# Sinks as a score column, split order of the first gate slot after an attention, and one product for a task's row numbers

## The reference

```python
def sink_softmax_values(s, sink, v):
    sk = jnp.broadcast_to(sink.astype(F32).reshape(1, KVC, REPC, 1, 1), s.shape[:-1] + (1,))
    p = jax.nn.softmax(jnp.concatenate([s, sk], axis=-1), axis=-1)[..., :-1]
    return jnp.einsum('bgrqk,bkgd->bqgrd', p.astype(v.dtype), v)

def merge_branches(h, oA, oB, oC, w_gate_l, w_branch_l, w_out_l):
    o = jnp.stack([oA, oB, oC], axis=2)
    p = jnp.einsum('btnc,ncd->btnd', o, w_branch_l)
    g = jax.nn.sigmoid((h @ w_gate_l).reshape(B, T, N_BRANCH, D_MODEL))
    return jnp.sum(g * p, axis=2) @ w_out_l

for e in range(N_EXP):
    y = y + gates[..., e:e + 1] * swiglu(h, w_ex_gate[i, e], w_ex_up[i, e], w_ex_down[i, e])
```

## Time and profile before

| | us |
|---|---|
| median of 3 runs | 1545.44 (1542.32 to 1548.37) |
| the profiled execution, its own time | 1546.68 |
| its span in the trace | 1544.3 |
| TensorE busy | 1490.6 (97%) |
| DVE busy | 944.2 (61%) |
| ACT busy | 787.4 (51%) |
| mean rate of transfers | 222 GB/s |

### The profile page before, as it was taken

How to read it: one execution, slowest core, us unless ns; L and a number is a source line. 1 busy time by engine, 2 the same in 40 slices (tenths; PEclk the granted TensorE clock), 3 DMA queues, 4 the chain that set the end, 5 groups by cost and what they waited for, 6 DMA issues and landing times.

```text
span 1544.3 us, 22244 instructions
## 1 busy us (share of the span) xinstructions
PE 1490.6 (97%) x8684; PEld 1312.1 (85%) x8684; DVE 944.2 (61%) x1133; ACT 787.4 (51%) x904; POOL 55.7 (4%) x54
## 2 busy tenths in 40 slices
PE   5999999999999999999999999998999999999997
PEld 4788969679999999997889696898888888888875
DVE  3642275655654254346522756556888898988988
ACT  4433263453532242234343544535778777787875
POOL 0100000000000000000000000000000000000002
PEclk8999999999999999999999999999999999999999
DMA  9754374573763444244333654534899999999994
GB/s 332 249 174 149 104 249 161 193 244 113 239 180 110 142 120 136 96 139 166 120 116 110 204 178 145 184 113 165 311 379 382 372 374 374 371 388 370 372 373 171
DMA packets 236028, 342.36 MB, mean 222 GB/s; under 512 B 8629, under 2 KB 156766, under 8 KB 235694
## 3 DMA queue, kind: packets, MB, share of 16 engines
q1 hardware_dynamic: 227392, 313.32, 59.3%
q0 software_dynamic: 6496, 24.69, 4.4%
q10 hardware_dynamic: 2062, 3.24, 0.6%
HBM read 325.74 MB, written 15.47 MB: 221 GB/s over the span
## 4 chain that ended last, share of the span: by engine, by line
PE 86%; DVE 6%; DMA 3%; ACT 3%; issue 1%; ACTq 0%; SPq 0%; DVEq 0%
PE ps L632 26%; PE ps L634 25%; PE ps L633 25%; PE ps L649 2%; DVE wlo L2004 2%; DMA raw<-in_w_ada_dram 2%; PE ps L809 1%; ACT whi L1439 1%; DMA raw<-in_w_gate_dram 1%; PE ps L681 1%; PE ps L1026 1%; DVE wlo L1625 1%; PE ps L715 1%; PE ps L826 1%; ACT whi L1208 0%
## 5 line engine op out<-in xcount | busy, mean ns | idle before, releaser
L632 PE MATMUL ps<-hhi,whi 128*128 128x384 f32 x864 | 291.1, 337 | 3.5 <-DVE wlo L1625 2.2
L634 PE MATMUL ps<-hhi,wlo 128*128 128x384 f32 x864 | 288.8, 334 | 0.0
L633 PE MATMUL ps<-hlo,whi 128*128 128x384 f32 x864 | 288.7, 334 | 0.0
L1625 DVE TENSOR_TENSOR wlo<-raw,whi 128x2048 fp32r<-128x2048 f32 x66 | 151.0, 2289 | 173.8 <-ACT whi L1208 173.5
L2004 DVE TENSOR_TENSOR wlo<-raw,whi 128x2048 fp32r<-128x2048 f32 (+1 forms) x81 | 179.7, 2228 | 28.6 <-ACT whi L1439 27.3
L1439 ACT ACTIVATE whi<-raw 128x2048 fp32r<-128x2048 f32 (+1 forms) x81 | 150.5, 1867 | 52.6 <-PE ps L634 52.3
L2004 DVE TENSOR_TENSOR wlo<-mraw,whi 128x2048 fp32r<-128x2048 f32 (+2 forms) x81 | 160.7, 1993 | 23.5 <-ACT whi L1439 23.1
L632 PEld LDWEIGHTS ps<-hhi,whi 128*128 128x128 f32 x864 | 162.2, 188 | 9.1 <-issue 3.2
L632 PE MATMUL ps<-whi,xgh 128*128 128x512 f32 (+1 forms) x432 | 163.8, 379 | 4.8 <-DVE wlo L2004 3.7
L633 PEld LDWEIGHTS ps<-hlo,whi 128*128 128x128 f32 x864 | 162.2, 188 | 0.3
L1439 ACT ACTIVATE whi<-mraw 128x2048 fp32r<-128x2048 f32 (+2 forms) x81 | 136.1, 1681 | 51.5 <-PE ps L634 51.1
(11 more groups left out here) (326 smaller groups left out, 2451.9 us busy)
## 6 DMA issues: line engine op xcount, KB each, us to landing
raw<-in_w_ada_dram SPq DMA_DIRECT2D x82, 512.0 KB, 5.7
raw<-in_w_ex_up_dram SPq DMA_DIRECT2D x27, 1024.0 KB, 7.4
raw<-in_w_ex_down_dram SPq DMA_DIRECT2D x27, 1024.0 KB, 6.6
raw<-in_w_gate_dram SPq DMA_DIRECT2D x48, 512.0 KB, 4.6
raw<-in_w_in_dram SPq DMA_DIRECT2D x44, 512.0 KB, 5.5
raw<-in_w_ex_gate_dram SPq DMA_DIRECT2D x18, 1024.0 KB, 7.3
mraw<-in_w_ex_gate_dram SPq DMA_DIRECT2D x18, 1024.0 KB, 7.9
mraw<-in_w_ex_down_dram SPq DMA_DIRECT2D x18, 1024.0 KB, 8.3
```

The lines of the kernel that those rows point to most:

```text
L632: pe.matmul(out, s[0], m[0], start=first, stop=False, **kw)
L633: pe.matmul(out, s[0], m[1], start=False, stop=False, **kw)
L634: return pe.matmul(out, s[1], m[0], start=False, stop=last, **kw)
L1625: dve.tensor_tensor(wlo[:, n % RING, :], raw[:, n % RING, :], whi[:, n % RING, :].bitcast(F32), ALU.subtract).then_inc(lo_done, 1)
```

## The change

Five edits.

1. *Sinks.* A new ACT step `sinks(l)`, after the last gate of branch 1, writes the eight sinks into spare columns of PSUM banks 0 to 3 with four instructions; TensorE waits for `sinks_set` before the first windowed scores. The scores of a step are placed so that the column of their sink is next to them (`score_col`, `with_sink`), the maximum and the exponentials run over 129 or 385 columns, and the sum contains the sink. L1788, L1789, L1349 and L1797 go. `ebuf` has 388 columns, and the weights start at column 1 or 257.
2. *Last exponentials.* `exps(11)` comes right after `pt_copy(9)`, before the output copy of the third head (before: after it).
3. *First gate slot.* ACT makes `whi` in two halves (`gate_hi`, one per block of 128 outputs), the first after `pt_copy(10)` (in layer 0's windowed attention after `pt_copy(11)`), the second after the last `pt_copy`; `whi` of the second gate slot comes behind `ada_end`. TensorE waits for the first half only (`gate_high`) and runs the first block as 16 products on `whi`, then, after `lo_done`, 8 on `wlo`.
4. *After a norm.* The first channel's products on `hhi` come first, behind `first_high`, and those on `hlo` after `first_ready`, in layer 1's input projection and in the dense SwiGLU.
5. *Row numbers.* The comparisons also multiply by the token number, DVE adds the three matrices, and TensorE makes one product with a column of ones.

```diff
+        def score_col(t):
+            return (1, 1, 122, 123)[t // 3] + (T - P if t % 3 == 0 and t else 0)
+        def weight_col(t):
+            return 1 + (T - P if t % 3 == 0 and t else 0)
+        def with_sink(c, t):
+            nk = P if t % 3 == 0 else T
+            return slice(c - 1, c + nk) if t < 3 else slice(c, c + nk + 1)
...
                 if l:
+                    pe.wait_ge(lo_done, split_count(win_slot(l, 0) + 1))
+                    pe.wait_ge(first_high, 2)
+                    w = [x[:, 0, :] for x in slot(win_slot(l, 0), 4)]
+                    for b in range(BLK):
+                        for half in range(2):
+                            pe.matmul(proj_out(Q_A)[:, b, :], hhi[:, 0, b * P:(b + 1) * P], w[half], start=(half == 0), stop=False)
                     pe.wait_ge(first_ready, 2)
-                    pe.wait_ge(lo_done, split_count(win_slot(l, 0) + 1))
                     for b in range(BLK):
-                        products(Q_A, b, (0,))
+                        pe.matmul(proj_out(Q_A)[:, b, :], hlo[:, 0, b * P:(b + 1) * P], w[0], start=False, stop=False)
...
+            def high_first(l, o, w, x):
+                out = ps[:, 2 * gate_pair(l, gate_slot(l, o, 0, 0)), 0:T]
+                pe.wait_ge(gate_high, 2 * l + o)
+                for k in range(KD):
+                    if o == 1 and k == 6:
+                        ada_end(2 + 2 * l)
+                    pe.matmul(out, w[0][:, k, 0:P], x[0][:, k, :], start=(k == 0), stop=False)
+                    pe.matmul(out, w[0][:, k, 0:P], x[1][:, k, :], start=False, stop=False)
+                pe.wait_ge(lo_done, split_count(gate_slot(l, o, 0, 0) + 1))
+                for k in range(KD):
+                    if o == 1 and k == 2:
+                        head_squares(l)
+                    pe.matmul(out, w[1][:, k, 0:P], x[0][:, k, :], start=False, stop=(k == KD - 1))
...
-                for b in range(BLK):
-                    mm = pe.matmul(ps[:, 7, 0:1], gat[:, b, :], slotc[:, 2 * P + b:2 * P + b + 1], start=(b == 0),
-                                   stop=(b == BLK - 1))
-                mm.then_inc(idx_mm, 1)
+                pe.matmul(ps[:, 7, 0:1], gat[:, 0, :], ones[:, 0:1], start=True, stop=True).then_inc(idx_mm, 1)
...
+            def gate_hi(l, o, j):
+                n = gate_slot(l, o, 0, 0)
+                if j == 0:
+                    raw_wait(act, n)
+                    if last_user(n, of_ada) >= 0:
+                        act.wait_ge(mm_done, last_user(n, of_ada) + 1)
+                dst, src = [x[:, n % RING, :].rearrange("p (k c) -> p k c", k=KD)[:, :, j * P:(j + 1) * P] for x in (whi, raw)]
+                act.activation(dst, src, copy).then_inc(hi_done if j else gate_high, 1)
...
+            def sinks(l):
+                act.wait_ge(gate_evac, 12 * l + 8)
+                for p in range(2):
+                    for hp, c in ((0, slice(0, T + 2, T + 1)), (2, slice(T + 122, T + 124))):
+                        x = act.activation(ps[:, 2 * p:2 * p + 2, c],
+                                           sinkr[:, l, 2 * hp:2 * hp + 4].rearrange("p (h m) -> p m h", m=2), copy)
+                x.then_inc(sinks_set, 1)
...
-                    if kind == 1:
-                        x = act.activation(small[:, p, 6:8], small[:, p, 4:6], ACT.Exp)
                     x.then_inc(e_done, 1)
...
                 for t in range(12):
-                    if t + 1 < 12:
+                    if t + 1 < 11:
                         exps(t + 1)
-                    if t == 10 and kind == 0:
-                        hi(gate_slot(l, 1, 0, 0))
                     pt_copy(t)
+                    if t == 9:
+                        exps(11)
                     if t % 3 == 0 and t >= 3:
                         o_copy(t // 3 - 1)
                     if t == 10 and kind == 1:
                         ada_rows(phase)
-                    if t == 11 and kind == 0:
-                        hi(gate_slot(l, 1, 0, 1))
-                    if t >= 10 and kind == 1:
-                        hi(gate_slot(l, kind + 1, 0, t - 10))
+                    if t == (11 if kind and l == 0 else 10):
+                        gate_hi(l, kind + 1, 0)
+                gate_hi(l, kind + 1, 1)
                 o_copy(3)
...
-                    x = dve.tensor_reduce(small[:, p, 0:2], ps[:, 2 * p:2 * p + 2, 0:nk], X, ALU.max, negate=True)
-                    if kind == 1:
-                        hp = t // 3
-                        link(x)
-                        link(dve.tensor_tensor(small[:, p, 0:2], small[:, p, 0:2], nsink[:, l, 2 * hp:2 * hp + 2], ALU.min))
-                        x = dve.tensor_tensor(small[:, p, 4:6], small[:, p, 0:2], sinkr[:, l, 2 * hp:2 * hp + 2], ALU.add)
-                    x.then_inc(nmax_done, 1)
+                    c = with_sink(score_col(t), t) if kind else slice(0, nk)
+                    dve.tensor_reduce(small[:, p, 0:2], ps[:, 2 * p:2 * p + 2, c], X, ALU.max, negate=True).then_inc(nmax_done, 1)
...
-            def slot_matrix(pos):
+            def token_matrix(pos, q):
                 for b in range(BLK):
-                    x = dve.tensor_scalar(gat[:, b, :], slotc[:, P:2 * P], pos(b), None, ALU.is_equal)
-                x.then_inc(gat_ready, 1)
+                    x = dve.tensor_scalar(gat[:, b, :], slotc[:, P:2 * P], pos(b), slotc[:, 2 * P + b:2 * P + b + 1],
+                                          ALU.is_equal, ALU.mult)
+                x.then_inc(token_part, 1)
+                dve.wait_ge(token_part, 2 * q + 1)
+                dve.tensor_tensor(gat[:, 0, :], gat[:, 0, :], gat[:, 1, :], ALU.add).then_inc(token_part, 1)
+                dve.wait_ge(token_part, 2 * q + 2)
+                dve.tensor_tensor(gat[:, 0, :], gat[:, 0, :], gat[:, 2, :], ALU.add).then_inc(gat_ready, 1)
```

More of the change, by code:

```diff
@@ L1122, in units @@
                         pe.wait_ge(unit_done, u * 8 + 2 * (s + 1))
-                        column(s, (0,))
+                        first_column(s, True)
+                    pe.wait_ge(first_ready, 1)
+                    for s in range(2):
+                        first_column(s, False)
                     for p in range(4):
@@ L1794, in normal @@
                     dve.wait_ge(e_done, st0 + t + 1)
[L1795 to L1797 removed]
+                    k0 = kind * weight_col(t)
+                    e = [ebuf[:, p, m, k0:k0 + nk] for m in range(2)]
                     link(dve.reciprocal(small[:, p, 8:10], small[:, p, 2:4]))
```

54 lines of the change are left out of this document (36 added, 18 removed).

## The result

The changed kernel took 1533.75 us in the median of five runs (1532.78 to 1535.22), the kernel before 1545.44 us (1542.32 to 1548.37) beside it: a ratio of 0.9919, 95% interval 0.9905 to 0.9934, so faster by 0.8%. On a second chip it was 1535.38 us against 1546.84, ratio 0.9925 (0.9913 to 0.9937). The prediction was 1534.7 us, range 1531 to 1541. The profiled execution took 1534.65 us, its span 1532.4 us; that of before was 12.0 us longer.

A forecast was written before the change was run, and what follows sets the result against it. TensorE, busy 97% of the span, was taken to bound the kernel. Terms 1.5 + 1.3 + 1.8 + 1.8 + 1.1 + 0.1 + 3.2 = 10.8 us off 1546.68 gave 1535.9, less 1.24 for the median: 1534.7 us, range 1531 to 1541.

The forecast's parts named there:

- Layer 0's first attention: At its end, last exponentials sooner and first gate products on high parts: gate starts at 228.4 instead of 229.90, 1.5 us.
- Layer 1's first attention: At its end, the same steps as in layer 0: gate starts at 887.05 instead of 888.34, 1.3 us.
- Layer 0's windowed attention: At its end, last copy before the split: gate at 322.5 instead of 324.68, 0.4 given back by late low part, 1.8 us.
- Layer 1's windowed attention: Gate at 975.15 instead of 976.96, 1.8 us; sinks as a column shorten waits between steps, 1.1 us (0 to 1.3).
- High parts after a norm: First products after a norm start on high parts: 0.1 us, bounded by 0 and 0.2.
- Row numbers: Expert tasks: four fp32 passes less, DVE's split some 0.1 us late; 0.40 us a task, 3.2 us, bounds 1.5 and 3.57.
- The signs: Gate 1.3 to 1.8 us after last transposes, no 0.3 us idle between layer 1's windowed steps, two passes, task 48.4 us.
- The scalings one element off: Attention weights start one element off; nothing lost expected, else two scalings a step cost 0.15 to 0.2 us more each.
- (a): Rival: the expert loop doesn't get faster, set by transfers or DVE's late split; 1537.9 us, chance 0.15.
- (b): Rival: the attentions give theirs back, half of 7.6 us is left; 1538.5 to 1540 us, chance 0.14.
- (c): Rival: TensorE was waiting for something else with the same end, nothing but noise; 1544 us, chance 0.05.
- (d): Rival, slower: DVE's token matrix delays the next split in 8 tasks, 2.4 us lost, 1540 with attentions' gain; chance 0.03.

The follow-up runs named there:

- rows_only: The kernel before with only the row numbers from one product (comparisons and two additions on DVE): 1544.41 us against 1546.92, ratio 0.9987; a task lasts 48.49 us.
- half_split: The changed kernel with the low part of each expert task's first slot made in two halves on DVE: 1533.84 us, ratio 0.9919 to the kernel before.
- norm_only: The kernel before with only the first products after a norm on high parts first: 1546.79 us, ratio 0.9997.
- short_loads: The changed kernel with only a quarter of each of twelve modulation slots transferred in layer 0's windowed attention: 1578.9 us, ratio 1.0206 to the kernel before.
- sinks_only: The kernel before with only the sinks as one more score column: 1544.95 us, ratio 0.9986.
- exps_only: The kernel before with only the last exponentials sooner: 1545.35 us, ratio 0.9987.

## Why the prediction was right, and where it was right by luck

The time came within 1 us of the forecast, and every part but the one after a norm went in the direction and by the mechanism told. But the sum of 10.8 us wasn't what the steps gave. Each run has its mean granted clock beside its time. Over the 163 runs of all these kernels, each against the mean of its own kernel, a run is 0.97 us longer for every 0.001 of clock that it lacks (correlation -0.84; in this fit the clock accounts for 70% of the scatter). Brought to a clock of 0.990 by that slope, the kernel before takes 1546.4 us (66 runs) and the changed one 1536.8 (11 runs): 9.7 +- 0.9 us (two standard errors). The touched steps show 9.8 us in the profiled pair; forecast were 10.8. The rest is clock: 0.9896 in the mean before, 0.9922 +- 0.0010 after. Without the correction the means of these runs are 12.2 us apart, and the medians of the first comparison 11.7. The prediction had no term for the clock, so that it hit the time within 1 us is luck: its sum was about 1 us too large and the clock gave 2 to 2.5. Whether that clock is chance or came with the change is open (last section). At equal clock the parts are 2.6 (rows), 5.0 (gate), 0.7 (sinks) and -0.2 (norm), each +- 0.7 to 0.9; of the gate's two edits the block alone is 4.3 and the exponentials 0.7. The four sum to 8.1; with these errors that and 9.7 are not told apart, and the traces put what the parts gain by each other at 0.4.

By its steps:

- *Layer 0's first attention, 1.5 us:* 1.5 at its end, right in this pair (1.3 to 1.8 against the other traces of the old order). One consequence was left out: the output copy now stands behind the moved exponentials, and TensorE waits for it (0.35 us by starts). Counted from the transposes before, the last ones come 0.57 us sooner instead of 0.77; the gate's first product follows them after 1.81 us instead of the 2.04 of the forecast, which paid for it.
- *Layer 1's first attention, 1.3:* 1.33.
- *Layer 0's windowed attention, 1.8 with 0.4 given back:* 2.2 at its end with 0.12 given back in the block, but 1.2 to 1.5 against the four other traces of the old order: the forecast was read from the one trace in which ACT waited for the gate slot. And 0.5 us of lead that came in from the first attention were gone at this one's last transposes, where the transfers set the pace (TensorE waited 2.8 us for them in this stretch, 2.1 before), and 0.3 more after it. The prediction knew that the transfers set the pace there and used it only for the sinks; the step before should have been asked the same. In this pair 3.3 us were forecast for layer 0 and 2.9 arrived, a difference that is smaller than what two traces of one kernel differ by there.
- *Layer 1's windowed attention, 1.8 + 1.1:* together 3.2 instead of 2.9: 1.38 and 1.40 alone, 0.42 more by both. These sizes were furthest off. The moved exponential was priced at 0.8 us at the last transposes and gives 0.27 as long as the small operations stand in the chain; the column was priced at 1.1 and gives 1.40.
- *High parts after a norm, 0.1:* nothing.
- *Row numbers, 0.40 a task:* 0.33 to 0.36, 2.7 us in all instead of 3.2. The prediction's own terms, 0.446 for four passes less 0.1 for the late split, give 0.35; the middle of 0.40 was set above them without a reason. From the product ahead of the token product to the one behind it were 0.813 us before and are 0.396 in the task shown, so 0.417 less with the late split in it; over the tasks looked at in three traces it is 0.375 to 0.458.
- *Heads' roots, 0.2 us of cover:* the reciprocal ends at 238.88, TensorE asks at 239.85: 1.0 us. *Sink writes, free:* four of 0.16 us each, done at 275.1, the scores start at 277.85.
- *The signs:* a gate 1.3 to 1.8 us behind the last transposes is what the first attentions show (1.81); in the windowed ones it is 2.9, as the prediction's own sum has it (322.5 against 319.53). One idle time above 0.3 us is left in layer 1's windowed attention, 0.38 at the last transposes. A task takes 48.50 us, not 48.4.

*The scalings one element off.* Of the changed kernel, groups by line and shape (us in all, mean ns, idle before): L1870 and L1871 start one element off, L1867 doesn't.

```profile
L1870 DVE TENSOR_SCALAR ebuf<-ebuf,small 128x384 f32<-128x384 f32 x16 | 6.8, 423 | 0.6
L1867 DVE TENSOR_SCALAR ebuf<-ebuf,small 128x384 f32<-128x384 f32 x16 | 6.7, 420 | 0.6
L1871 DVE TENSOR_SCALAR ebuf<-ebuf,small 128x384 f32<-128x384 f32 x16 | 6.7, 416 | 0.0
```

423 and 416 ns against 420: nothing is lost. The Trainium skill ("Vector Engine (DVE) Microarchitecture Reference", section 5.1) asks for an even outermost dimension for the doubled rate of one-source operations in SBUF and says that 4-byte alignment makes no difference. The trace agrees in that the shifted start costs nothing; but one fp32 element is 4 bytes, so a start off a 4-byte boundary was not tried here.

*The rivals.* (a) is out by `rows_only`; a task of 48.33 us in `half_split` moves the same bytes again faster, 379 GB/s. The limit of about 358 GB/s for one core, which the Trainium skill gives as half of a stack's 716 GB/s ("DMA: Bandwidth & Descriptors", Where 436 GB/s comes from), is passed by this program, which runs on one core: the measurement decides. (b) happened at most in part: 0.8 us of lead were lost in layer 0, within what traces of one kernel differ by. (c) is out: the gains at layer 1's attentions stand in every trace that has the edits. (d): once DVE's cover is used up all of it counts, 0.97 us of DVE work for 0.97 us a task.

## What to carry to other kernels

Where two chains meet at one point (the weights of the last step and the split for the next product), an edit of either is worth only what the other leaves, and both together can be worth more than their sum (3.20 against 1.38 and 1.40 us here): cost them together. Where a stretch waits for transfers, its length differs between traces of one kernel by as much as such an edit gives, so read the gain from the steps that repeat and from several traces. A lead that enters a stretch paced by transfers can be lost there, so ask that of the step that made it. And before calling 2 us a gain, look at TensorE's clock in the two traces: here the two traces of the changed kernel have 0.991 and 0.989, which is 2 us by the slope above.

## What the runs showed of the hardware

TensorE's granted clock falls to 1.2 GHz in the start, in the sums and small products of a norm, and at the end. In twelve traces of nearly the same program the stretch near 695 us lasts 3.4 or 6.8 us, and those near 300, 411, 975 and 1060 us are there or not.

Whether the change has a part in it is open. The 86 runs of kernels with the old attentions (before, rows_only, norm_only) have a mean clock of 0.9897 +- 0.0004, the 38 with all the edits 0.9915 +- 0.0006, which would be 1.8 us. (short_loads, whose run is longer, is among the 38; without it they have 0.9913.) That is more than the scatter from run to run explains, but no run tried a cause by itself. On the second chip, in one comparison, the gap is smaller: 0.9901 before against 0.9911 to 0.9915 in the four kernels beside it.

One cause can be looked at in the traces. The only two falls inside layer 0's windowed attention, in rows_only and norm_only, begin at 298.7 and 298.4 us. Just ahead of them, at 297.6 and 297.7, TensorE had waited 2.0 and 2.6 us for a modulation transfer, the longest such waits in this stretch of any trace here. The old order alone doesn't make that fall: before, sinks_only and exps_only have none there. The fall near the end of layer 1's windowed attention (from 974.2) stands in norm_only alone, and the waits ahead of it, 0.85 and 0.89 us, are those of before, where the clock held. Three falls are few.
